# The sums of squares of x by four narrow column groups and a summing product, instead of sixteen whole products

## What is computed

```python
def _rms(x, g):
    xf = x.astype(jnp.float32)
    y = xf * lax.rsqrt(jnp.mean(xf * xf, axis=-1, keepdims=True) + EPS)
    return (y * g.astype(jnp.float32)).astype(x.dtype)

c_act = jax.nn.silu(c)
mod = c_act @ w_ada[l] + b_ada[l]
shift, scale, gate = jnp.split(mod, 3, axis=-1)
h = _rms(x, norm_g[l]) * (1.0 + scale[:, None, :]) + shift[:, None, :]
proj = h @ w_in[l]
```

## Time and profile before

| | |
|---|---|
| median of 3 runs | 2800.1 us (2796.76 to 2800.23) |
| profiled execution, its own time | 2796.65 us |
| its span | 2795.3 us |
| TensorE busy | 2747.3 us, 98% |
| VectorE, ScalarE, GpSimd busy | 1042.5, 1054.7 and 1244.4 us |
| DMA | 323.31 MB, 116 GB/s in the mean |

### The profile page before, as it was taken

The page is one execution under the profiler, slowest core; times in us unless marked ns, Lnnn a source line. Parts: engine busy times, 40 slices in busy tenths (PEclk is TensorE's granted clock), DMA queues, the critical chain, the costliest instruction groups (busy, mean ns, idle before and its releaser), DMA issues.

```text
span 2795.3 us, 31839 instructions
## 1 busy us (share of the span) xinstructions
PE 2747.3 (98%) x12680; PEld 2226.1 (80%) x12680; DVE 1042.5 (37%) x1690; ACT 1054.7 (38%) x1726; POOL 1244.4 (45%) x631
## 2 busy tenths in 40 slices
PE   7999999999999999999999999999999999999999
PEld 5878888887778778878887777777878888888787
DVE  5866645643122122134576332333222222212300
ACT  4224334333333333234443444444443444433311
POOL 3634334434334335454344333444455555555543
PEclk9789999999999999999999999999999999999999
DMA  9853333222222224432222222222233333333343
GB/s 369 285 178 122 113 111 122 103 72 72 87 91 80 87 91 140 143 109 83 79 80 83 91 87 94 87 95 94 95 114 103 115 104 118 116 112 122 127 143 109
DMA packets 102963, 323.31 MB, mean 116 GB/s; under 512 B 11424, under 2 KB 14496, under 8 KB 102304
## 3 DMA queue, kind: packets, MB, share of 16 engines
q1 hardware_dynamic: 99072, 307.64, 31.9%
q10 hardware_dynamic: 3744, 13.63, 1.4%
HBM read 304.45 MB, written 16.78 MB: 115 GB/s over the span
## 4 chain that ended last, share of the span: by engine, by line
PE 88%; DVE 5%; DMA 2%; POOL 2%; ACT 1%; issue 1%; SPq 0%; DVEq 0%; ACTq 0%; POOLq 0%
PE bank L742 26%; PE bank L744 25%; PE bank L743 25%; PE bank L945 2%; PE bank L933 2%; PE bank L864 2%; DVE TA L1703 1%; POOL wlo L1883 1%; DMA TA<-in_strip 1%; PE bank L925 1%; PE bank L792 1%; DVE TA L1398 1%; DMA TA<-in_w_ada 1%; PE bank L692 1%; ACT whi L1002 1%
## 5 line engine op out<-in xcount | busy, mean ns | idle before, releaser
L1883 POOL TENSOR_TENSOR wlo<-wraw,whi 128x1024 fp32r<-128x1024 f32 (+2 forms) x454 | 1049.3, 2312 | 1364.7 <-ACT whi L1002 1364.3
L742 PE MATMUL bank<-Hhi,whi 128*128 128x512 f32 x2928 | 1199.0, 410 | 9.4 <-DVE Hlo L1858 3.5
L744 PE MATMUL bank<-Hhi,wlo 128*128 128x512 f32 x2928 | 1147.4, 392 | 0.0
L743 PE MATMUL bank<-Hlo,whi 128*128 128x512 f32 x2928 | 1147.1, 392 | 0.0
L1002 ACT ACTIVATE whi<-wraw 128x1024 fp32r<-128x1024 f32 (+2 forms) x454 | 457.3, 1008 | 709.0 <-PE bank L744 677.1
L742 PEld LDWEIGHTS bank<-Hhi,whi 128*128 128x128 f32 x2928 | 553.2, 189 | 149.0 <-issue 26.0
L743 PEld LDWEIGHTS bank<-Hlo,whi 128*128 128x128 f32 x2928 | 553.5, 189 | 118.6 <-issue 10.8
L744 PEld LDWEIGHTS bank<-Hhi,wlo 128*128 128x128 f32 x2928 | 552.4, 189 | 119.5
L742 PE MATMUL bank<-Ohi,whi 128*128 128x512 f32 x320 | 128.8, 403 | 0.0
L743 PE MATMUL bank<-Olo,whi 128*128 128x512 f32 x320 | 124.8, 390 | 0.0
L744 PE MATMUL bank<-Ohi,wlo 128*128 128x512 f32 x320 | 124.8, 390 | 0.0
(11 more groups left out here) (237 smaller groups left out, 2661.6 us busy)
## 6 DMA issues: line engine op xcount, KB each, us to landing
wraw<-in_w_in SPq DMA_DIRECT2D x304, 512.0 KB, 3.2
TA<-in_w_ada SPq DMA_DIRECT2D x64, 512.0 KB, 5.7
Y<-in_w_ada SPq DMA_DIRECT2D x32, 512.0 KB, 4.4
wraw<-in_w_out SPq DMA_DIRECT2D x32, 512.0 KB, 3.2
wraw<-in_w_o SPq DMA_DIRECT2D x32, 512.0 KB, 3.2
wraw<-in_w_mem ACTq DMA_DIRECT2D x16, 512.0 KB, 6.9
tmp_mgs<-TA SPq DMA_DIRECT2D x32, 256.0 KB, 2.1
TA<-tmp_mgs SPq DMA_DIRECT2D x32, 256.0 KB, 3.6
```

Of the source, the lines that this page charges most:

```text
L742: e.matmul(out, hi[:, c], xhi[k], start=first and j == 0, stop=False)
L743: e.matmul(out, hi[:, c], xlo[k], start=False, stop=False)
L744: m = e.matmul(out, lo[:, c], xhi[k], start=False, stop=last and end)
L1883: e.tensor_tensor(M.wlo[b][:, 0:w], M.wraw[b][:, 0:w], M.whi[b][:, 0:w].bitcast(F32), ALU.subtract).then_inc(S.lo)
```

## The change

TensorE no longer has a pair of products in each of items 0 to 7. In items 1, 3, 5 and 7 it has four: buffer g of M.xsq is multiplied by 32 columns of ones into the partitions 32g to 32g+31 of the bank. After item 7 each group of 32 partitions holds the sum over four of the sixteen pieces. ScalarE copies the bank into M.xsq[1] (new semaphore xsum4), and in item 8, behind its twelve products, TensorE multiplies that by the whole matrix of ones into the same bank. As each partial sum stands there 32 times, Ln has the scale 1/(32 D).

```diff
--- before.py
+++ after.py
@@ -373,7 +373,7 @@
         self.msq, self.mg, self.mst, self.rr = sem("msq"), sem("mg"), sem("mst"), sem("rr")
         self.mkv, self.mks, self.mkn, self.mkr = sem("mkv"), sem("mks"), sem("mkn"), sem("mkr")
         self.mkm, self.mkt, self.mkk = sem("mkm"), sem("mkt"), sem("mkk")
-        self.xsq, self.xst, self.xr = sem("xsq"), sem("xst"), sem("xr")
+        self.xsq, self.xst, self.xsum4, self.xr = sem("xsq"), sem("xst"), sem("xsum4"), sem("xr")
         self.xnv, self.xnp, self.hs = sem("xnv"), sem("xnp"), sem("hs")
         self.adm, self.adq, self.adc, self.adp = sem("adm"), sem("adq"), sem("adc"), sem("adp")
 
@@ -663,10 +663,14 @@
                 e.matmul(out, xlo[k][:, c], hi[:, w], start=False, stop=False)
                 m = e.matmul(out, xhi[k][:, c], lo[:, w], start=False, stop=k == KT - 1)
         m.then_inc(S.item)
-        if k < 8:
-            for x in (2 * k, 2 * k + 1):
+        if k in (1, 3, 5, 7):
+            for g in range(4):
+                x, r = 2 * k - 2 + g, slice(32 * g, 32 * g + 32)
                 pe.wait_ge(S.xsq, x + 1)
-                e.matmul(M.bS0, ones, M.xsq[x % 4], start=x == 0, stop=x == KT - 1).then_inc(S.xst)
+                e.matmul(M.bS0[r, :], ones[:, 0:32], M.xsq[g], start=k == 1, stop=k == 7).then_inc(S.xst)
+        if k == 8:
+            pe.wait_ge(S.xsum4, 1)
+            e.matmul(M.bS0, ones, M.xsq[1], start=True, stop=True).then_inc(S.xst)
         ada(range(3 * k, 3 * k + 3))
         if k == 6:
             totals(0)
@@ -1048,7 +1052,9 @@
             put("mem", k + 8, M.memt, k + 8, ("mg", k + 9), None)
         if k == 8:
             act.wait_ge(S.xst, KT)
-            e.activation(M.xr, M.bS0, ACT.Ln, scale=1.0 / D, bias=M.eps).then_inc(S.xr)
+            e.activation(M.xsq[1], M.bS0, ACT.Copy).then_inc(S.xsum4)
+            act.wait_ge(S.xst, KT + 1)
+            e.activation(M.xr, M.bS0, ACT.Ln, scale=1.0 / (32 * D), bias=M.eps).then_inc(S.xr)
             act.wait_ge(S.xr, 1)
             e.activation(M.xr, M.xr, ACT.Exp, scale=-0.5).then_inc(S.xr)
         if k >= 12:
```

## The result

| | before | after |
|---|---|---|
| median of 6 runs | 2799.11 us | 2807.67 us |
| lowest and highest | 2796.76 to 2802.56 | 2805.29 to 2811.26 |
| ratio | | 1.0031, 95% interval 1.0018 to 1.0044 |
| profiled execution, its span | 2795.3 us | 2807.6 us |

The changed kernel is slower by 8.6 us. The same kernel timed again beside other runs gave a ratio of 1.0026 (1.0017 to 1.0035). I had forecast plus 5.3 us, which is under the 5.6 us that I set as the bound of a difference, and a range of 2799.0 to 2811.0. The time lies in the range, but both measurements lie over that bound, and two terms of the sum were far off, with opposite signs. The profiles show it line by line.

A forecast was written before the change was run, and what follows sets the result against it. From 80 to about 139 us VectorE's queue, started by xr, was taken as critical. Minus 3.44 + 1.29 + 5.85 + 1.6 gave plus 5.3 us on 2800.1, forecast 2805.4 us, range 2799.0 to 2811.0.

The forecast's parts named there:

- The path: From 80 to about 139 us VectorE's queue is critical; a later xr (factor 1/rms of x) moves everything by as much.
- my own sign: Prediction wrong if VectorE's first product with xr starts before 81 or after 90 us, or PE's first h part doesn't follow.
- The late sum: Summing product behind item 8's twelve products, in front of Ln: 4.99 + 0.86 = plus 5.85 us.
- What is removed before 43.26 counts nothing: Pairs of items 0 and 2 are free, the L692 behind item 2's still waiting for its DMA until 41.45 us.
- The quad: Four narrow products replacing a pair in items 3, 5 and 7: 2.15 us each against 1.72, plus 1.29 us in all.
- My bound of 3.44: Upper bound in us for a quad, its four narrow products running one behind another; the lower bound was 0.86.
- the wholly-side-by-side one: Rival: column groups overlap fully, quad 0.86 us; xr minus 0.2 to plus 3.0 us, time 2801.5 us; chance 0.27.
- the page's second one: Skill page's statement that matmuls start and end in program order; the reason given for not taking a quad of 0.87 us.
- The clock: Items 3, 4, 6 and 8 lose 0.8 us each, 3.2, of which 1.6 was paid before: plus 1.6 us, ends 0 and 3.2.
- minus 3.44: Removed pairs of items 4 and 6, on the path: 2 x 1.72 us saved.
- the one without overlap: Rival: column groups don't overlap, quad 3.44 us; plus 9.2 us, time 2809.3 us, slower; chance 0.30.
- no change and slower: Outcomes split at 5.6 us (0.2%): no change, chance 0.52, and slower, chance 0.42.

The follow-up runs named there:

- all three kernels that had the fill: Changed kernel plus two useless whole products in item 2 (ratio 1.0014), in items 2, 4 and 6 (1.0019), or the latter with the sum in item 7 (1.0002).

## Why the prediction was right or wrong

**The path** was right: xr through VectorE's fixed order to PE's wait. The first product with xr moved by 12.0 us, that wait by 11.0, the last sums by 9.2, the median by 8.6. The forecast passed the shift on in full; the runs show 1 to 3 us of it lost on the way, which the text had not counted. By my own sign (wrong if that first product starts after 90 us) the prediction failed in the first profile, 92.00, and not in the second, 88.79. The summing product was to stand at 83 to 85 us and stood at 89.56 and 86.35. PE's idle time up to the wait for w_ada went from 20.3 to 27.9 us (136.34 less 116.01 busy, 147.31 less 119.43), up by 7.5 where I had said some 9.

**The late sum**, plus 5.85 us, was right: 5.7 by the run that has it alone.

**What is removed before 43.26 counts nothing** was wrong. Item 2's pair lay beside a DMA wait, so its time was free, but it was what kept PE at work in that time. Without it PE sat idle for 3.51 us and came back slow: its w_ada products ended 1.66 us later (44.92 against 43.26), and item 3's products took 2.97 us more. Filling the gap gave that back, in all three kernels that had the fill.

**The quad**, 2.15 us, was wrong: 0.99. The reason, that the second record of a product must follow the first and records start in order, does not hold the groups apart: the trace has four records starting at once and the other four together behind them (last section). Three quads were worth minus 2.2 us, not plus 1.29. A change to narrow groups and back costs besides: the quads at 65.70 and 83.46 start 0.33 and 0.32 us behind the start of the record ahead of them, where 0.23 is usual, and the w_ada products behind a quad take 1.81 us (66.69 to 68.50) instead of 1.70. That is the 0.1 us a switch which I had left in the range, twice for each quad, 0.6 us in all. My bound of 3.44, "the change doesn't do what it says", is out; of the rivals the wholly-side-by-side one had the mechanism right, and its 0.86 nearly. By the Trainium skill's first statement ("TensorE: Matmul & The Clock Gate", Part 3) a quad would be 0.87; the trace has 0.99, nearer to it than to my reading of the page's second one.

**The clock**, plus 1.6 us with 3.2 as its end, was the step that failed most. With the measured values of the other terms, minus 3.44 - 2.2 + 5.85, the 12.0 us leave 11.8 for it, and the 8.8 us of the second profile leave 8.6; the 0.6 us of the switches are in both. The granted clock by itself gives nearly the same, 13.7 and 10.1 less the 1.8 of before, so 11.9 and 8.3. I had priced an item without a pair by items 8 to 11 (0.8 us lost in each), and counted four of them. In the windows from 40 to 80 us the clock was 1.00 and 0.91 before, and 0.66 and 0.72 after: with 1.2 GHz as half, a mean of 0.66 means that PE ran at the lower level for 68% of the time, and 0.72 for 56%, not for 0.8 us in four of them. The run with eight products less shows it without the change: 5.4 us of work taken away, nothing won. So the minus 3.44 and minus 2.2 were not to be had on this path. What failed is the step from items 8 to 11 to the items after the change: the loss in an item isn't a price that can be carried over and multiplied, and the runs don't show a rule for where the clock falls.

The two errors of size, minus 3.5 us for the quads and plus 7 to 10 for the clock, left the sum at plus 5.3 for xr, where 12.0 and 8.8 were measured, and for the time, where 8.6 and 7.0 were. That the time lies in the range is luck: the range reached so far up for a rival whose mechanism is out, and part of the shift was lost on the way. That this rival, the one without overlap, gave nearly the measured time (2809.3) is chance too. The decision between no change and slower (0.52 to 0.42) hung on the clock term, and it went to slower.

## What to carry to other kernels

In this kernel work taken from TensorE was worth its time only where the clock stayed up. Look at the granted clock of the stretch, and ask whether the products that go are what keeps it there. Ask it also of products that are free because they lie beside a wait; here they were the reason that the work behind the wait was fast. And a sum that is split to go faster needs a last step: place that step where its inputs are ready and not behind the next block of the in-order queue.

## What was not expected of the hardware

Eight whole products of the kernel before cut to one column (5.4 us of PE less) left its time as it was (ratio 1.0001), and two useless ones put into a DMA wait brought the changed kernel from ratios of 1.0031 and 1.0026 to 1.0014 (the intervals overlap a little).

Four f32 products of 128x512 into four groups of 32 columns took 0.99 us at a granted clock of 2.4 GHz, where two whole ones take 1.72. How they lie is to be seen in the changed kernel. The first two rows have the least, the median and the greatest duration (ns) of the loads and of the records of all quads. The third has all loads of the quad of item 5, and the fourth is PE's row of that quad in a timeline that ends at 65.90 us.

```profile
L670 PEld LDWEIGHTS bank<-first,cst x32: 106/109/154, 31.6 to 83.5; 128*32 128x32 f32 x32
L670 PE MATMUL bank<-first,cst x32: 592/605/802, 31.6 to 83.9; 128*32 128x512 f32 x32
65.69 0.16 PEld L670 LDWEIGHTS bank<-first,cst 128*32 128x32 f32 x8 [0.36 <-issue]
65.70 0.64 PE L670 MATMUL bank<-first,cst 128*32 128x512 f32 x4
```

Eight loads take 0.16 us together, where one takes 0.109, so the loads run side by side and don't set the pace. Four records have started before 65.90 and take 0.64 us together, where one takes 0.62 by itself. The other four start only after 66.10, which is one step of a whole record (0.43 us) later. So the quad is two rounds of four records side by side, 0.87 us, and 0.1 us at its end until the next product starts. Such a quad of f32 products into four column groups runs side by side in full, though each product is two records into the same columns.

Why the clock's slow stretches fell differently in two executions of the same program (first product with xr at 92.00 and 88.79) is open.
